# Tile 0's expert choice in two stages: VectorE ranks a head's pairs, GpSimd finds the experts' numbers

## What is computed

```python
q = (hb @ w_q).astype(f32).reshape(PEER_BLOCK, PEER_HEADS, 2, PEER_QDIM // 2)
s = jnp.einsum('nhpd,pkd->nhpk', q, sub_keys.astype(f32))
s_half, i_half = lax.top_k(s, PEER_TOPK)
cand = (s_half[:, :, 0, :, None] + s_half[:, :, 1, None, :]).reshape(PEER_BLOCK, PEER_HEADS, PEER_TOPK * PEER_TOPK)
cid = (i_half[:, :, 0, :, None] * PEER_NKEYS + i_half[:, :, 1, None, :]).reshape(PEER_BLOCK, PEER_HEADS, PEER_TOPK * PEER_TOPK)
best_s, best_j = lax.top_k(cand, PEER_TOPK)
eid = jnp.take_along_axis(cid, best_j, axis=-1)
gate = jax.nn.softmax(best_s, axis=-1)
act = jax.nn.gelu(jnp.einsum('nd,nhkd->nhk', hb.astype(f32), u_tab[eid].astype(f32)))
out = jnp.einsum('nhk,nhkd->nd', gate * act, v_tab[eid].astype(f32))
```

## Time and profile before

| | |
|---|---|
| median of 3 runs | 2725.84 us (2725.48 to 2734.8) |
| the profiled execution: its own time | 2723.77 us |
| the profiled execution: span from first to last instruction | 2722.0 us |
| busy: TensorE / VectorE / ScalarE / GpSimd | 71% / 40% / 16% / 29% of the span |
| moved by DMA | 920.20 MB, 338 GB/s on the mean |

### The profile page before, as it was taken

How to read it: one execution, slowest core, us unless ns; L and a number is a source line. 1 busy time by engine, 2 the same in 40 slices (tenths; PEclk the granted TensorE clock), 3 DMA queues, 4 the chain that set the end, 5 groups by cost and what they waited for, 6 DMA issues and landing times.

```text
span 2722.0 us, 30506 instructions
## 1 busy us (share of the span) xinstructions
PE 1919.9 (71%) x11817; PEld 1239.2 (46%) x11817; DVE 1096.2 (40%) x1921; ACT 438.7 (16%) x975; POOL 790.5 (29%) x595
## 2 busy tenths in 40 slices
PE   5799999988898953676749897672764216655673
PEld 1477777868768952565636564121221201111120
DVE  2200002415564397676660127028777850000014
ACT  0100000122162221434400101111221100000011
POOL 1000000000000027443452223337966842222224
PEclk9799999989869985787869999766987556677785
DMA  9789996343027689999999999999999999999997
GB/s 384 278 316 333 346 326 229 124 124 124 11 87 224 211 276 415 412 413 411 412 421 413 414 415 417 415 399 405 400 386 409 357 411 404 401 418 421 421 421 318
DMA packets 284430, 920.20 MB, mean 338 GB/s; under 512 B 22383, under 2 KB 158627, under 8 KB 210107
## 3 DMA queue, kind: packets, MB, share of 16 engines
q0 software_dynamic: 78384, 569.78, 51.3%
q1 hardware_dynamic: 177506, 313.16, 32.2%
q10 hardware_dynamic: 28396, 35.35, 3.6%
HBM read 909.57 MB, written 17.21 MB: 340 GB/s over the span
## 4 chain that ended last, share of the span: by engine, by line
DMA 39%; PE 12%; POOL 9%; DVE 8%; issue 3%; ACT 0%; ACTq 0%; POOLq 0%; DVEq 0%; PEldq 0%
DMA sb_ring<-in_peer_v_dram,sb_modT 20%; DMA sb_ring<-in_peer_u_dram,sb_dist 15%; POOL sb_ring L2610 9%; DVE sb_ring L2102 4%; PE ps L2532 3%; DMA sb_ring<-in_cache_sel_kv_dram 2%; PE ps L1855 2%; PE ps L2288 1%; PE ps L2259 1%; DMA sb_pT<-in_cache_sel_kv_dram 1%; DVE sb_work L2034 1%; PE ps L995 1%; PE ps L1698 1%; DVE sb_work L2031 1%; PE ps L1999 1%
## 5 line engine op out<-in xcount | busy, mean ns | idle before, releaser
L2102 DVE SCALAR_TENSOR_TENSOR sb_ring<-sb_ring,sb_pT 128x2048 f32<-128x2048 f32 x264 | 602.8, 2295 | 211.5 <-DMA sb_ring<-in_peer_u_dram,sb_dist 197.5
L2610 POOL DMA_INDIRECT sb_ring<-in_peer_u_dram,sb_dist x256 | 476.0, 1859 | 477.8 <-DVE sb_ring L2102 294.2
L2532 PE MATMUL ps<-sb_ring,sb_xT 128*32 128x512 f32 x2048 | 343.4, 764 | 214.3 <-DMA sb_ring<-in_peer_v_dram,sb_modT 211.4
L2610 POOL DMA_INDIRECT sb_ring<-in_peer_v_dram,sb_modT x256 | 254.7, 995 | 583.6 <-PE ps L2532 561.0
L418 PE MATMUL ps<-sb_hT,sb_ring 128*128 128x264 f32 x1664 | 374.8, 387 | 0.0
L418 PEld LDWEIGHTS ps<-sb_hT,sb_ring 128*128 128x128 f32 x1664 | 314.8, 190 | 66.0 <-issue 13.0
L2532 PEld LDWEIGHTS ps<-sb_ring,sb_xT 128*32 128x32 f32 x2048 | 49.8, 121 | 445.4 <-DMA sb_ring<-in_peer_v_dram,sb_modT 400.4
L2367 PE MATMUL ps<-sb_ident,sb_ring 128*128 128x128 f32 x512 | 103.7, 361 | 138.5 <-DMA sb_ring<-in_cache_cmp_kv_dram 111.3
L1657 PE MATMUL ps<-sb_work,sb_pT 128*64 128x512 f32 x160 | 98.1, 700 | 91.1 <-ACT sb_work L1545 59.2
L2367 PEld LDWEIGHTS ps<-sb_ident,sb_ring 128*128 128x128 f32 x512 | 78.6, 185 | 161.4 <-DMA sb_ring<-in_cache_cmp_kv_dram 131.6
L2421 ACT ACTIVATE sb_pT<-ps 128x256 f32<-128x256 f32 x256 | 127.2, 659 | 100.8 <-PE ps L2367 100.7
(11 more groups left out here) (575 smaller groups left out, 2431.8 us busy)
## 6 DMA issues: line engine op xcount, KB each, us to landing
sb_ring<-in_w_ada_dram SPq DMA_DIRECT2D x48, 2048.0 KB, 10.9
sb_ring<-in_w_in_dram SPq DMA_DIRECT2D x26, 2048.0 KB, 14.1
sb_ring<-in_w_out_dram SPq DMA_DIRECT2D x19, 1024.0 KB, 10.4
sb_ring<-in_peer_wq_dram SPq DMA_DIRECT2D x18, 1024.0 KB, 12.3
sb_ring<-in_cache_cmp_kv_dram SPq DMA_DIRECT2D x68, 256.0 KB, 11.8
sb_ring<-in_w_out_dram SPq DMA_DIRECT2D x8, 2048.0 KB, 8.6
sb_ring<-in_cache_cmp_kv_dram ACTq DMA_DIRECT2D x60, 256.0 KB, 9.4
sb_pT<-in_peer_wq_dram SPq DMA_DIRECT2D x14, 1024.0 KB, 15.8
```

Source lines behind the costliest of these rows:

```text
L2102: dve.scalar_tensor_tensor(R3(rows), R3(rows), 1.0, h2r[t] if t < NT else R3(h2w), ALU.mult, ALU.mult, accum_out=(dots if t < NT else dots ...
L2532: mm = pe.matmul(bank(G % 2)[32 * q:32 * q + 32, :], w, rows[:, 512 * q:512 * q + 512], start=j == 0, stop=j == last)
L2610: pool.indirect_dma_start(rbuf[e % NBUF], None, io["peer_u" if kind == "u" else "peer_v"][0], bass.IndirectOffsetOnAxis(index, 0)).then_in ...
```

## The change

For tile 0, `dve_head` now ends with the two ranks of the chosen pairs, which it writes into one of two buffers `ints0` and reports with `pairs_ranked`. From the third head on it waits, ahead of that write, until the numbers of the head two before are found. The lookup is a new function `pool_lookup` on GpSimd: one head's work is 12 instructions, most of which wait for the one before. The comparison is a subtraction and a test for zero, and the sum over 16 is a tree of four additions. `pool_gather` calls it for head 0 ahead of the first gathers, for heads 1 to 6 ahead of gather 4, and for head 7 ahead of gather 6. The semaphore `ids_here` goes.

```diff
+        ints0 = [ints, v3(work, 416, 2, TOPK)]
+        pick2 = v4(work, 1024, 2, TOPK, TOPK)
...
-            mark(c, dve.tensor_copy(topf[0:r], U32v(topi[t][0:r, 2 * h:2 * h + 2])))
+            if t:
+                mark(c, dve.tensor_copy(topf[0:r], U32v(topi[t][0:r, 2 * h:2 * h + 2])))
...
             ji = I32v(bestj[t][0:r, h])
+            if t == 0:
+                if h >= 2:
+                    dve.wait_ge(sem("experts_ready"), h - 1)
+                dve.tensor_scalar(I32v(ints0[h % 2][:, 0]), ji, 4, None, ALU.logical_shift_right).then_inc(sem("pairs_ranked"), 1)
+                dve.tensor_scalar(I32v(ints0[h % 2][:, 1]), ji, 15, None, ALU.bitwise_and).then_inc(sem("pairs_ranked"), 1)
+                return
...
-            if t == 1 and h == 0:
+            if h == 0:
                 dve.wait_ge(sem("ids_T"), 1)
...
+            dve.wait_ge(sem("experts_ready"), HEADS)
             for h in range(HEADS):
                 dve.wait_ge(sem("keyscores"), HEADS + h + 1)
...
-            pe.wait_ge(sem("ids_here"), t + 1)
             pe.wait_ge(sem("experts_ready"), HEADS * (t + 1))
...
+        def pool_lookup(pool, h):
+            c = sem("peer_consts")
+            pool.wait_ge(sem("pairs_ranked"), 2 * h + 2)
+            mark(c, pool.tensor_copy(topf, U32v(topi[0][:, 2 * h:2 * h + 2])))
+            step(pool, c, pool.tensor_copy(halves, I32v(ints0[h % 2])))
+            one_hot = pick2.rearrange("p i j k -> p (i j) k")
+            step(pool, c, pool.tensor_tensor(one_hot, B2(halves.rearrange("p i j -> p (i j)"), TOPK), B1(iota16, 2 * TOPK), ALU.subtract))
+            step(pool, c, pool.tensor_scalar(one_hot, one_hot, 0.0, None, ALU.is_equal))
+            step(pool, c, pool.tensor_tensor(pick2, pick2, topf.unsqueeze(2).to_broadcast([P, 2, TOPK, TOPK]), ALU.mult))
+            for w in (8, 4, 2, 1):
+                dst = one_hot[:, :, 0:w] if w > 1 else ids.rearrange("p i j -> p (i j)").unsqueeze(2)
+                step(pool, c, pool.tensor_tensor(dst, one_hot[:, :, 0:w], one_hot[:, :, w:2 * w], ALU.add))
+            mine = slice(h * TOPK, (h + 1) * TOPK)
+            step(pool, c, pool.tensor_scalar(ids[:, 0], ids[:, 0], float(NKEYS), None, ALU.mult))
+            step(pool, c, pool.tensor_tensor(eid_rows[:, mine], ids[:, 0], ids[:, 1], ALU.add))
+            pool.tensor_copy(I32v(eid[:, mine]), eid_rows[:, mine]).then_inc(sem("experts_ready"), 1)
+
         def pool_gather(pool):
+            pool_lookup(pool, 0)
             pool.wait_ge(sem("proj_sum"), 8 + 68)
             for e, (kind, t, n) in enumerate(ENTRIES):
                 if e == 4:
+                    for h in range(1, HEADS - 1):
+                        pool_lookup(pool, h)
                     pool.wait_ge(sem("proj_sum"), 8 + 84)
+                if e == NBUF:
+                    pool_lookup(pool, HEADS - 1)
```

More of the change, by code:

```diff
@@ L75 @@
     top_ready exp_done pt_part dve_steps samp_consts samp_ready x1_ready keys_T keys_ready rows_out
-    rows_mm keyscores keyscore_mm halves_done top_diff peer_consts experts_ready ids_here keys_in
+    rows_mm keyscores keyscore_mm halves_done top_diff peer_consts experts_ready pairs_ranked keys_in
     rest_in0 w2b_in
@@ L2089, in dve_queries @@
                 dve_head(dve, P, 0, h, [ks0[h % 2][:, half] for half in range(2)])
-            dve.sem_inc(sem("ids_here"), 1)
             dve_differences(dve, 0)
```

## The result

The changed kernel takes 2751.95 us in the median of 7 runs (2746.46 to 2760.81), the kernel before 2725.84 in 7 runs beside them: a ratio of 1.0087, with a 95% interval of 1.0066 to 1.0108, so 18 to 29 us slower; 2745 us were predicted. The profiled execution took 2748.23 us, its span is 2746.5 us, 24.5 us above that of before.

A forecast was written before the change was run, and what follows sets the result against it. From about 1015 us a gapless DMA stream bounds the kernel, so its start sets the end; 965.9 + 8 x 6.85 + 5.1 + 2.5 = 1028.3 us against 1007.55, 20.7 later on 2723.8, gives 2745 us (range 2731 to 2758).

The forecast's parts named there:

- What bounds the kernel: From about 1015 us a gapless stream of bytes; what starts it later moves the end by the same amount.
- The queue's opening: GpSimd's list ahead of the lookups: not free before about 965.9 us, since its semaphore clearing waits for SyncE.
- The lookup: Twelve GpSimd instructions per head of tile 0: 6.85 us each, between 5.1 and 8.0, eight on the path.
- VectorE as follower: VectorE's ranking in tile 0 doesn't set the pace: 6.3 us a head, below the lookup's 6.85.
- worth 24 us: VectorE's share in tile 0: the 3 us a head that go, if nothing took their place on the path.
- Blocking: What GpSimd's lookup loses beside VectorE's ranking: 0.15 us a lookup taken, from nothing to 0.76.
- The rival that blocking takes 8 us or more for a lookup: Engines block each other during lookups: at 8.0 us each the time is 2754 us; 10 in 100 above 8.0.
- The late scores: ScalarE's last scores and SyncE's page loads come at about 990 us for 986.19; costed at nothing.
- A cheap lookup: Rival: second operand free, lookup 5.1 to 5.9 us, time 2730 to 2737 us, within 0.5%; 16 in 100.
- The delay was carried to the end: Rival denied here: slack later in the stream keeps time near 2726 us; 6 in 100 together with VectorE as pace.
- The rival that VectorE becomes the pace: Lookups of 3.4 us let VectorE set the pace: 2723 us; 6 in 100 together with delay not carried on.
- this change could hardly win 0.5%: Even a lookup that costs nothing gains only 10 us, 0.4%; faster by over 0.5% got 2 in 100.

The follow-up runs named there:

- subtraction twice: Changed kernel with the subtraction of each lookup (128x512, two operands) issued twice: 2760.75 us, 1.0133 of the kernel before.
- three before the clearing: Changed kernel with the lookups of heads 0 to 2 ahead of GpSimd's wait and semaphore clearing: 2730.43 us, 1.0016 of the kernel before.
- three heads moved: Against the kernel before, only heads 3 to 5 have their lookup on GpSimd, with own rank buffers: 2721.31 us, ratio 0.9981.
- one more multiplication: Changed kernel with a multiplication by 1.0 ahead of each lookup's test for zero: 2768.04 us, 1.0152 of the kernel before.
- leaving the lookup out: Changed kernel without comparison, product and tree of sums (7 of 12 instructions), output different: 2724.85 us, 0.9996 of the kernel before.

## Why the prediction was right

**What bounds the kernel** held for a later start. The stream of bytes is the same behind its start, and over four kernels from -5.3 to +35.2 us at the first dot (changed, subtraction twice, three before the clearing, three heads moved) the median followed within 1 us, which is closer than the intervals, 4 to 7 us to either side, can vouch for; with one more multiplication it followed within 4. In the profiled executions the time from the first dot to the end is 1713.0 to 1717.0 us over all starts from before's to 38.4 us later, so a delay is carried on. For the two kernels that start earlier it is 1719.0 and 1720.4 us, so in those executions the gain was lost on the way. What took it stays open.

**The queue's opening** held. With GpSimd's 112.12 us of idle time before it, the first cast came at 961.31 in an execution that was 4.8 us ahead of that of before, so at 966.1 on its clock; 965.9 was taken. That the queue opens late was an inference from SyncE's rows; three lookups before the clearing show it, with 21.5 us less in the median.

**The lookup** was the mis-sized term: 6.85 us reckoned, 7.4 measured. By its parts, each with its gap, from the second lookup's rows: both casts 0.44; the subtraction 1.18 and the product 1.35, where 1.28 each was reckoned; the test for zero 1.60 for 0.79; the tree 2.01 for 1.97; the last three 0.76 for 0.84. The one-operand price was wrong, because I took it from rows of another instruction (AFFINE_SELECT). The two-operand price, built on the same rows and a difference of 30 ns, came out by luck: that a second operand adds to the time of one is not what the rows show, since the test with one operand is slower than the subtraction and the product with two. The test alone is 0.8 us too much in each lookup, and 6.5 us in eight; smaller gaps and casts, and less blocking than the 0.15 us reckoned, gave 2 back, which leaves 4.4 = 8 x 0.55. The rest of the miss is the way from a lookup to the first gather, 0.90 us idle ahead of 969.66, so 5.9 us for gathers 0 to 3 where 5.1 was reckoned. 20.7 + 4.4 + 0.8 = 25.9, the measured shift; smaller differences of 0.1 to 0.2 us cancel out.

The Trainium skill's GPSIMD Engine Reference, section 3.1, has 4497 ns for two operands of 2048 elements, which is 2.2 ns per element and an estimate of 1.12 us for 512; 1.09 and 1.26 were measured, so the trace agrees. The Trainium skill's same page, section 4.1, calls work with one input "roughly line-rate", against about two times slower than VectorE with two; the 1.50 us for 512 elements are 2.9 ns per element, which is slower than two operands here, and the measurement decides.

**VectorE as follower** held: it waited at the end of each head from head 2 on, and it never set the pace. Beside the lookups its heads took 7.1 us, not 6.3 (7.39 from 989.55 to the same instruction of the next head at 996.94, less 0.30 of wait), so it came close to it. What the prediction calls worth 24 us was never to be had, though, for VectorE can't rank faster than the scores come. In the kernel before ScalarE copied them out 7.6 to 8.5 us apart for heads 0 to 6, and the last head's here:

```profile
985.14 0.38 ACT L1988 ACTIVATE sb_work<-ps 128x256 f32<-128x256 f32 x1 [0.80 <-PE ps L1979]
```

With 6.3 us of ranking behind it, the last ranks could have come at 991.8 at the earliest, by this estimate 16 us ahead of 1007.55. In the changed kernel the same limit shows as the waits of 2 us ahead of heads 1 and 2.

**Blocking** was priced at 0.15 us a lookup. GpSimd lost less: its tree takes 1.93 us beside an idle VectorE and 1.99 to 2.00 beside the ranking. VectorE lost more than I had looked at: the addition of pairs takes 1.26 us beside a lookup, 0.42 without (972.15), but it had time to lose. The Trainium skill's rule (SBUF — State Buffer, section "Who interferes with whom") fits: the addition has two SBUF inputs, and it ends just behind GpSimd's product beside it (985.47 + 1.26 = 986.73, against 985.18 + 1.26 = 986.44). The rival that blocking takes 8 us or more for a lookup did not come about.

**The late scores** held: SyncE's first page loads were issued at 988.39, which is 993.2 on the clock of before (this execution was 4.8 us ahead of it). That is 7 us later than the 986.19 of before, where 4 were reckoned. They still were done by 1010, 19 us ahead of the dots, and cost nothing.

**The rivals.** A cheap lookup fell with the measured 7.4 us. The delay was carried to the end. The rival that VectorE becomes the pace was reached by leaving the lookup out: the dots were 6.3 us earlier, close to the reckoning, and 0.2% of the time, so nothing here goes against the claim that this change could hardly win 0.5%.

## What to carry to other kernels

Work that moves to an idle engine is free only if that engine's queue is open when the work becomes ready, and only if it is through before the results are needed: here eight lookups of 7.4 us behind a queue that opened at 966 us replaced 3 us a head. Look for what the queue must do first (here a clearing that waits for all engines), and move only as many pieces as fit into the time that the other engine has: three of eight gained about 5 us (0.8 to 9) where eight lost 26. And price an instruction from rows of its own kind, since a neighbour's row missed by a factor of two.

## What the runs showed of the hardware

GpSimd's TENSOR_SCALAR with 128x512 float32 took 1.50 us, with a multiplication as with a test, 2.9 ns per element, while its TENSOR_TENSOR of that size took 1.09 us with two broadcast operands and 1.26 in place with one broadcast operand. Beside a lookup on GpSimd, 128x256 VectorE instructions with two SBUF operands took 0.88 to 1.26 us (additions) and 1.48 us (a product) for 0.42, and an int32 TENSOR_SCALAR of 16 elements 0.87 for 0.17, while GpSimd's own instructions grew by no more than 0.2 us in the rows looked at.
